# A two-layer transformer kernel whose attention stages are dealt out by TensorE tile shape, with masks added ahead of key products

## The reference

```python
def hybrid_layer(x, ...):
    (sb_q, sb_k, sb_v, nsa_q, ck, cv, sk, sv, wk, wv, nsa_g, mb_q, mb_k, mb_v, merge_g) = jnp.split(x @ w_in, ...)
    o_sb = stick_breaking_attention(...)     # 4 heads; every key before the query
    o_nsa = nsa_attention(...)               # 4 heads, one shared key head: compressed + 8 chosen blocks of 64 + window 512
    o_moba = moba_attention(...)             # 4 heads, one shared key head: own block of 256 + the 3 best of the past
    g = jax.nn.sigmoid(merge_g).reshape(B, S, N_BRANCHES, D)
    mix = g[:, :, 0] * (o_sb @ w_br_sb) + g[:, :, 1] * (o_nsa @ w_br_nsa) + g[:, :, 2] * (o_moba @ w_br_moba)
    x = layer_norm(DEEPNORM_ALPHA * x + mix @ w_out, ln1_g, ln1_b)
    return layer_norm(DEEPNORM_ALPHA * x + peer_ffn(x, ...), ln2_g, ln2_b)

def peer_ffn(x, w_q, sub_k1, sub_k2, u_tab, v_tab):   # for 128 tokens at a time
    q = ...; s1, s2 = q[..., :half] @ sub_k1, q[..., half:] @ sub_k2     # 4 heads x 128 keys, twice
    idx, g = ...                                      # top 8 of each, top 8 of their 64 sums, softmax
    act = jax.nn.gelu(jnp.einsum('thkd,td->thk', u_tab[idx], xb))
    return jnp.einsum('thk,thkd->td', g * act, v_tab[idx])
```

## Time and profile before

| | us |
|---|---|
| median of 3 runs | 2829.38 |
| lowest and highest run | 2827.62, 2830.81 |
| the profiled execution: span from first to last instruction | 2819.9 |
| TensorE busy | 2453.4 |
| VectorE busy | 1942.6 |
| GpSimd busy | 1233.1 |
| ScalarE busy | 786.9 |

### The profile page before, as it was taken

The page is one execution under the profiler, slowest core; times in us unless marked ns, Lnnn a source line. Parts: engine busy times, 40 slices in busy tenths (PEclk is TensorE's granted clock), DMA queues, the critical chain, the costliest instruction groups (busy, mean ns, idle before and its releaser), DMA issues.

```text
span 2819.9 us, 30185 instructions
## 1 busy us (share of the span) xinstructions
PE 2453.4 (87%) x10632; PEld 1484.2 (53%) x10632; DVE 1942.6 (69%) x4009; ACT 786.9 (28%) x1563; POOL 1233.1 (44%) x1028
## 2 busy tenths in 40 slices
PE   8998998998999989899988887999989999987126
PEld 4764476575445357657654465476445347644012
DVE  0122245588988875667886887587998886687875
ACT  2243222213344332321342212212445333301001
POOL 0000023354565432434553655164656352656775
PEclk9998999999989999999997998999999899999569
DMA  4323258787888776977896999787889685998998
GB/s 144 105 73 100 90 188 337 273 290 253 304 283 302 266 251 224 379 286 270 323 359 246 338 375 350 272 297 255 298 297 330 221 308 200 394 366 317 362 373 320
DMA packets 224183, 776.98 MB, mean 276 GB/s; under 512 B 23200, under 2 KB 39712, under 8 KB 219552
## 3 DMA queue, kind: packets, MB, share of 16 engines
q0 software_dynamic: 147456, 536.94, 52.1%
q1 hardware_dynamic: 73696, 227.80, 22.6%
q10 hardware_dynamic: 2880, 10.31, 0.9%
HBM read 766.56 MB, written 8.39 MB: 275 GB/s over the span
## 4 chain that ended last, share of the span: by engine, by line
PE 57%; DVE 15%; DMA 9%; issue 8%; POOL 7%; ACT 3%; another core or an unknown queue 0%; DVEq 0%; ACTq 0%; SPq 0%
PE ps L1056 14%; PE ps L931 7%; PE ps L900 6%; PE ps L984 6%; PE ps L1089 5%; POOL rows L840 4%; DVE x L1535 4%; DMA rows<-in_table_u,idx 4%; PE ps L886 3%; DMA rows<-in_table_v,idx 3%; PE ps L1124 3%; DVE rows L1520 2%; PE ps L1150 2%; DMA wring<-in_merge 2%; PE ps L993 2%
## 5 line engine op out<-in xcount | busy, mean ns | idle before, releaser
L840 POOL DMA_INDIRECT rows<-in_table_u,idx x462 | 565.2, 1223 | 1021.3 <-DVE idx L1643 506.7
L1056 PE MATMUL ps<-xT,wring 128*128 128x256 f32 x3072 | 768.1, 399 | 56.5 <-DMA wring<-in_merge 24.6
L840 POOL DMA_INDIRECT rows<-in_table_v,idx x434 | 526.5, 1213 | 490.5 <-DVE x L1535 362.4
L1056 PEld LDWEIGHTS ps<-xT,wring 128*128 128x128 f32 x3072 | 586.2, 197 | 245.4 <-issue 90.4
L1520 DVE CUSTOM_DVE_ANT_0 rows<-rows,x 128x1024 f32<-128x1024 f32 x462 | 555.0, 1223 | 120.0 <-DMA rows<-in_table_u,idx 114.3
L1535 DVE SCALAR_TENSOR_TENSOR x<-rows,wts,x 128x1024 f32<-128x1024 f32 x413 | 529.8, 1283 | 65.6 <-DMA rows<-in_table_v,idx 43.6
L1089 PE MATMUL ps<-KA,QA 33*128 33x512 f32 (+7 forms) x576 | 253.7, 537 | 26.5 <-DVE part_m L1777 12.9
L1389 ACT ACTIVATE scratch<-scratch,negm 128x640 f32<-128x640 f32 (+7 forms) x192 | 143.5, 747 | 475.3 <-DVE negm L1777 464.6
L900 PE MATMUL ps<-wring,G 128*128 128x512 f32 x384 | 184.8, 617 | 9.7 <-DVE G L1678 6.3
L1777 DVE CUSTOM_DVE_ANT_0 scratch<-ps,cst 128x128 f32<-128x128 f32 (+3 forms) x192 | 86.9, 454 | 143.0 <-PE ps L1089 140.3
L886 PE MATMUL ps<-oT,wring 128*128 128x256 f32 x384 | 126.0, 464 | 53.0 <-DVE G L1673 35.1
(11 more groups left out here) (209 smaller groups left out, 2951.4 us busy)
## 6 DMA issues: line engine op xcount, KB each, us to landing
wring<-in_merge SPq DMA_DIRECT2D x216, 512.0 KB
wring<-in_w_out_h SPq DMA_DIRECT2D x48, 512.0 KB
wring<-in_w_query SPq DMA_DIRECT2D x32, 512.0 KB
G<-in_w_query SPq DMA_DIRECT2D x12, 1024.0 KB, 8.5
G<-in_x SPq DMA_DIRECT2D x16, 512.0 KB, 4.6
G<-in_ln SPq DMA_DIRECT2D x8, 1024.0 KB, 6.8
G<-x_mid SPq DMA_DIRECT2D x16, 512.0 KB, 5.4
rows<-in_table_u,idx POOLq DMA_INDIRECT x462
```

The source lines that it names most:

```text
L840: pool.indirect_dma_start(row_slot(n), None, tab_u if table == "u" else tab_v, bass.IndirectOffsetOnAxis(ap=idx[:, GT * (g % 2) + t, e:e + ...
L1056: mm = pe.matmul(gate_bank(p)[:, SW * n:SW * (n + 1)], w[:, lo:lo + P], xT[:, kc, SW * (p // HALF_GATES):SW * (p // HALF_GATES + 1)], star ...
```

## The change

Within each phase the streams are no longer sorted by place. `deal` takes one step at a time from the streams' heads, the one with the smallest place, where a head that keeps the array's present shape, or that uses no TensorE, counts as 4.0 weight units (of the phase's total) nearer. Each stream keeps its own order. `tile_shapes` says which shape a step enters with and leaves with; turns count as whole.

In a `keys` step the masks are written first (start=True) and the key products are added to them, so the step ends in the 64x128 shape. The sums are the same.

`expert_shares` prices TensorE anew: the factors go from 1.12, 1.0 and 1.1 to 0.98, 0.9 and 1.02, and 0.2 us is added for each change of shape. Expert steps therefore stand elsewhere: 839 in place of 840 before the tail, and within group 1 they go from 73, 45, 58 and 50 (phases 0 and 1 together, 2, 3, 4) to 64, 41, 55 and 65; in group 3 from 73, 45, 58 and 55 to 64, 41, 55 and 75.

```diff
+def deal(streams, i0):
...
+    out, shape, nxt = [], WHOLE, [0] * len(placed)
+    while any(n < len(own) for n, own in zip(nxt, placed)):
+        heads = []
+        for k, own in enumerate(placed):
+            if nxt[k] < len(own):
+                at, st = own[nxt[k]]
+                first = tile_shapes(st, i0)[0]
+                heads.append((at - (FAVOUR / work if first in (None, shape) else 0.0), k))
+        k = min(heads)[1]
...
+        shape = tile_shapes(st, i0)[1] or shape
+    return out
...
-        out += [st for _, _, _, st in sorted(placed, key=lambda a: a[:3])]
+        out += deal(streams, GT * half)
...
-            now += (.78 if kind in HEAD_KINDS or s < 0 else 1.12 if not late else 1.0 if g % 2 else 1.1) * pe
+            if kind in HEAD_KINDS or s < 0:
+                now += .78 * pe
+            else:
+                first, last_ = tile_shapes(what, GT * (g % 2))
+                now += (.98 if not late else .9 if g % 2 else 1.02) * pe
+                if first is not None:
+                    now += SHAPE_US * ((first != shape) + (first != last_))
+                    shape = last_
...
                         for n, (branch, b) in enumerate(jobs):
+                            if b == i or (branch == "win" and b == i - 4):
+                                mask = M_KEEP if b == i else M_EDGE
+                                pe.matmul(bank(2 + n).rearrange("p (h q) -> p h q", h=NH), masks[:, M_ID:M_ID + P],
+                                          masks[:, mask:mask + P].unsqueeze(1).to_broadcast([P, NH, P]),
+                                          start=True, stop=False, skip_group_check=True)
+                        for n, (branch, b) in enumerate(jobs):
+                            masked = b == i or (branch == "win" and b == i - 4)
...
-                            mm = pe.matmul(bank(2 + n), k, q, start=True, stop=True, skip_group_check=True)
-                        for n, (branch, b) in enumerate(jobs):
...
+                            mm = pe.matmul(bank(2 + n), k, q, start=not masked, stop=True, skip_group_check=True)
```

More of the change, by code:

```diff
@@ L228, in head_steps, with tile_shapes @@
     return steps
+ROW_TILE, COLUMN_TILE, WHOLE = "64x128", "128x32", "128x128"
+FAVOUR = 4.0
+def tile_shapes(step, i0):
+    kind, t, a, _ = step
+    if kind in ("zc", "score"):
+        return ROW_TILE, ROW_TILE
+    if kind == "keys":
+        i = i0 + t
+        masked = any(b == i or (br == "win" and b == i - 4) for br, b in key_jobs(i)[a])
+        return WHOLE if masked else ROW_TILE, ROW_TILE
+    if kind in ("cmp", "values", "sticks"):
+        return COLUMN_TILE, COLUMN_TILE
+    if kind in ("weigh", "log_sum", "soft", "spread", "tanh", "mean", "norm", "route"):
+        return None, None
+    return WHOLE, WHOLE
+def deal(streams, i0):
+    placed, work = [], sum(st[3] for _, steps, _ in streams for st in steps)
+    for begin, steps, span in streams:
+        whole, at, own = sum(st[3] for st in steps), 0.0, []
+        for st in steps:
+            own.append((begin + span * at / whole, st))
+            at += st[3]
+        placed.append(own)
+    out, shape, nxt = [], WHOLE, [0] * len(placed)
[7 more added lines that the diff above has]
+        k = min(heads)[1]
+        st = placed[k][nxt[k]][1]
+        nxt[k] += 1
+        out.append(st)
+        shape = tile_shapes(st, i0)[1] or shape
+    return out
 def steps_of(g):
@@ L348, in expert_shares @@
     out, times, now, busy, nxt, ready, started, ahead, late, landed = {}, [], 0.0, 0.0, 0, 0, 0.0, EXPERT_AHEAD, False, 0.0
+    shape = WHOLE
     for g in range(NG + 1):
@@ L386, in expert_shares @@
     return out, times
-EXPERT_US, EXPERT_AHEAD, TIGHT_AHEAD = 1.33, 3.0, -0.5
+EXPERT_US, EXPERT_AHEAD, TIGHT_AHEAD, SHAPE_US = 1.33, 3.0, -0.5, 0.2
 SPREAD, ROUTED, ROW_US = .8, [], 1.9
```

5 lines of the change are left out of this document (removed).

## The result

| | before | after |
|---|---|---|
| median of the runs, us | 2830.1 | 2893.99 |
| lowest and highest, us | 2827.62, 2864.1 | 2891.31, 2895.95 |
| ratio after/before, 95% interval | | 1.0207 [1.0152, 1.0262] |
| span of the profiled execution, us | 2819.9 | 2893.0 |

The account below looks back on a forecast made before the run. TensorE was taken to set the pace in all four attention stages, with the last stretch fixed. The terms −77 −10 +35 +19 +6 +3 gave −24 us, so 2805 us was forecast, range 2762 to 2842.

Parts of the forecast that it names:

- Switches −77: TensorE's order in the attention stages: 384 fewer changes of tile shape at 0.20 us each save 76.8 us.
- concurrent scores −10: Moba and window scores on different array rows run side by side on TensorE, at 52 places: 10 us saved, bounds 0 and 15.
- (D): Rival: switches aren't what costs; same-row steps still expose weight loads, 0.10 us saved per switch, 2844 us; chance 0.02.
- Score waits +35: Runs of scores outrun two banks and wait for VectorE's reads: 35 us more, bounds 12 and 66.
- Half clock +19: Groups 1 and 3: TensorE runs at half clock behind new score waits, 19 us lost, bounds 0 and 53.
- Merges +6: Merge steps drawn together wait for their one bank: 6 us more, bounds 0 and 16.
- Ring of weights +3: Gate steps wait for weights by DMA, an eighth more than before: 3 us, bounds 0 and 12.
- Copies 0: ScalarE's copies and exponentials cost TensorE nothing more, as ScalarE is 28% busy: 0 us.
- Expert steps 0: VectorE's expert work is moved, not added, and the last phase of group 1 has room: 0 us.
- (C): Rival: slower, VectorE's reads pace the score runs because expert steps keep it behind; up to 2880 us; chance 0.17.
- (A): Rival: waits hardly grow, since VectorE is relieved in heavy phases; −72 us, 2757 us; chance 0.16.
- (B): Rival: nothing is left, no gain from score pairs and score waits at 51 us; +2, 2831 us; chance 0.09.

Follow-up runs that it names:

- e7: The change with its reach FAVOUR cut from 4.0 to 1.0, so steps are taken less far ahead; ratio to the kernel before 0.9960.
- e1: The change with the planner's old prices of TensorE and nothing for a shape change; dealt order and masks kept; ratio to the kernel before 1.0286.
- e16: The change, favouring only steps of another kind than the last, the spread step taken early, FAVOUR 2.0; ratio to the kernel before 0.9953.
- e13: The change, but a shape-keeping step is favoured only if of the same kind as TensorE's last step; ratio to the kernel before 1.0284.
- e10: The change, but a shape-keeping step is favoured only if of another kind than TensorE's last step; ratio to the kernel before 1.0027.
- e4: The change, but zc and score steps are never dealt early for their shape; ratio to the kernel before 1.0075.
- e2: The kernel before with the planner's new prices alone, its order and masks unchanged; ratio to the kernel before 0.9967.
- e5: The kernel before with VectorE's two expert operations cut from 1024 to 64 columns; ratio to the kernel before 0.9954.
- e6: The changed kernel with VectorE's two expert operations cut from 1024 to 64 columns; ratio to the kernel before 1.0172.
- e3: The kernel before with the masks written ahead of the key products and nothing else; ratio to the kernel before 0.9992.
- e11: The kernel before with VectorE's expert operations cut to 64 columns and every score bank read twice; ratio to the kernel before 1.0088.

## Why the prediction was wrong, point by point

**What bounds the kernel: right.** TensorE sets the pace in the attention stages, after as before; all of the loss shows as its idle time and its half clock.

In the attention stages −24 us were forecast and +64 measured. The 88 us between them are three steps: the saving was sized too large (32 us), idle time was sized too small (34), above all by a term put at nothing, and with it the half clock (22).

**Switches −77 and concurrent scores −10: mis-sized, both together −55.** For 384 switches that is 0.14 us each, pairs included. Other deals give 0.12 (e7), 0.15 (e1, e16), 0.16 (e13) and 0.18 (e10). The step that failed is "the two joined scores show the full 0.20": one sort of joint, score to score, was taken for all. The rival (D) had 0.10 us for each switch. The Trainium skill, TensorE: Matmul & The Clock Gate, "The mechanism" (Part 3), says that a weight load overlaps matmuls in flight only where the row groups differ; the 0.10 is the prediction's own split of its rows by that rule. The measured mean lies between that and 0.20, so 2 in 100 was too little for its size. Its mechanism is not shown: no run here separates the two ends of a switch.

**Score waits +35: size about right (+27), by luck, since the cause was wrong.** The prediction said that "inside a run the two keep step" and that only the first wait is late, "by what VectorE has in hand then". With VectorE's load halved the waits grow nearly as much (+21), and with VectorE idle the third score of a run still waited 0.42 us. It is the round trip of a bank, and it was there in the first rows: two banks, a product, a read of 0.75 us and two hand-overs.

**Half clock +19: measured +41, inside its bounds of 0 to 53.** The rate was taken per waiting score, and other waits had been left out. Half clocks come without runs of scores too: e4 has +25 with +54 of idle time.

**Merges +6: +10 in the attention stages. Ring of weights +3: +2.4.** Both near. The sign named for merges, waits near 41 us, was not seen (34.0), as their waits in the heads shrank.

**Copies 0 and other kinds 0: the term that was missing.** "ScalarE is 28% busy" was the reason to cost the rest at nothing. This is the step that failed with the most behind it. Load was the wrong view: the gate has its bank copied by ScalarE, and its wait for that went from 19.6 to 32.3 us; suffix, match, keys, stick, out and query steps added 28 us, the turns in the heads 11. TensorE's idle time grew by 78 us in the attention stages and 85 in all, against 44 in the forecast. The prediction listed only the kinds for which the trace of before already showed large waits (scores, merges, gates on weights). But the old order had kept most steps apart from their own kind (222 neighbours of a kind, 430 after), which is the likely reason why their waits weren't in that trace.

**Expert steps 0: nearly.** By e2 their new places gain 0.3%, and by e5 and e6 their load is not what the change loses by. **The last stretch fixed: nearly,** +3.7 us.

**The rivals.** (C), slower, was right in its sign, and in its title, "VectorE's reads pace the runs", for the scores; it was wrong in its reason, the expert steps. Its 2880 comes within 14 us by luck: it had score waits at +66 (measured +27) and the half clock at +53 (+41), which stood in for the waits of other kinds that it left out too. Of its two signs one was seen, attention stages of groups 1 and 3 that gained nothing, and the other not, waits for the reads past 70 us (48.9). It had been given 0.17. (A) and (B) fell. In numbers for the attention stages: forecast −87 +44 +19 = −24; measured −55 +78 +41 = +64.

## What to carry to other kernels

An order of work that looks untidy may be what hides the hand-back of buffers. Before steps are sorted by a likeness such as tile shape, count how often a step comes to stand behind one that uses its own bank or buffer, for every kind and not only for those that wait now, and price each by the full round trip: product, reader, hand-over. Favour likeness only between steps that share nothing, and look afterwards for the one step whose input has slipped behind a long operation of another engine: here it alone cost 0.8%.

## What the runs showed of the hardware

Each change of tile shape removed took 0.12 to 0.18 us off TensorE's busy time, in the mean over 168 to 384 of them, scores that run side by side included; that is less than the 0.20 us read from single places. Four profiles with the old order and masks last or first (e2, e3, e5, e11) differ from before by −3 to +5 us in the same measure. VectorE's multiply-add over 128x1024 took 1.28 us; cut to a sixteenth of the columns three of them in a row took 1.06 us, 0.35 each, so a good part of the price doesn't shrink with the width:

```profile
690.99 1.06 DVE L1585 SCALAR_TENSOR_TENSOR x<-rows,wts,x 128x64 f32<-128x64 f32 x3
```

And VectorE's fall from 69% to 35% busy, with TensorE setting the pace, gave 0.5%.
